# A hybrid decoder layer: order of the attention steps on four engines, and where the large buffers begin in on-chip memory

## The chip, the core and the metric

The kernel runs on one core of a Trainium2 chip. The metric is the device time of one execution in microseconds (us). Weights and activations come from HBM by DMA, work happens in SBUF (128 partitions, each with its own byte addresses), and TensorE writes its results to PSUM, which has eight banks of 2 KB in each partition.

## The reference, cut to what matters

One layer over 512 tokens of width 1024, all float32:

```
h    = RMSNorm(x)
proj = h @ w_in          # RWKV part | q | k | v | gate_A | gate_B
y_a  = rwkv7(...) @ w_up_a            # chunked recurrence, 8 heads of 64
y_b  = causal attention with ALiBi(q, k, v) @ w_up_b   # 8 heads of 64
x    = x + (sigmoid(gate_A) * y_a + sigmoid(gate_B) * y_b) @ w_o
h    = RMSNorm(x)
x    = x + (silu(h @ w_g) * (h @ w_u)) @ w_ffn_out     # hidden width 2816
out  = RMSNorm(x)
```

With 512 tokens and blocks of 256, at most one block is fully past, so the block-sparse attention is plain causal attention.

## The kernel before, in words

**Products in three parts.** Every large product is kept near float32 accuracy by splitting both operands into a rounded part (`_hi`) and a rest (`_lo`), both of type float32r. `three` (L1481) issues hi*hi (L1483), hi*lo (L1484) and lo*hi (L1485) into the same PSUM bank, each a matmul of 128 rows by 512 moving columns. The first operand of `pe.matmul(out, a, b)` is the stationary one (a weight load, LDWEIGHTS in the trace, goes ahead of each matmul), the second is the moving one. The names in a row of the trace are not in that order. One matmul loads 512 bytes of each partition as its stationary operand and streams 2,048 bytes of each partition as its moving one.

**Weight units.** The weights come in 147 units of 128x1024, numbered by stage: 3 LoRA units (the second and third with 80 columns a tile instead of 128), 12 for r, k, v, 4 for the attention's values (VB), 8 for its q and k (QK), 16 gate units (`U_GATE`), 8 up units, 8 for w_o, 44 for the FFN's first product, 22 for its second. SyncE (SP) loads a unit into `wraw` (2 slots, L454), ScalarE (ACT) rounds it into `w_hi` (`split_hi`, L755), VectorE (DVE) makes `w_lo` (`split_lo`, L1096; both with 4 slots), and TensorE takes it (`take`, L1498). A unit of the gates, LoRA, RKV, QK and the FFN's first product is 24 matmuls with `w` stationary and `hT` (the transposed h) moving. The VB units have `hT` stationary and `w` moving. The up stage (L1899) has `w` stationary and `yaT` or `obT` moving. w_o (`by_rows`, L1909) has `mixT` stationary and `w` moving; the FFN's second product (`down`, L1944) has `act` stationary and `w` moving.

**The attention stage** has 16 steps n, for four pairs of heads times four query tiles t = n mod 4 of 128 tokens. One gate unit goes with each step. In a step:
- `attn_scores` (L1820): two matmuls (four records in the trace) with 128(t+1) moving columns;
- DVE `score_bias` (L1348) adds the ALiBi row and keeps the maximum, ACT `probs` (L998) does the exponential and the sum, DVE `weights` (L1360) takes the reciprocal and scales;
- `probs_T` (L1838): 2(t+1) transposes, read out of PSUM by ACT's `probs_T` (L1008) into `PT`;
- `values` (L1849): the product with V, 4(t+1) records;
- `gate` (L1863): a half of the unit (12 matmuls) into PSUM bank 0, from which DVE `gate_copy` (L1374) copies the result. The first half of the next unit waits for that copy (L1870).
- at the end of four steps ACT's `ob_hi` (L1017) and DVE's `ob_lo` (L1369) take the pair's result out of bank 1.

The order is written out by hand for each engine. TensorE (L1880 to L1894) issues, in step m: first gate half, scores of m+1, transposes of m, second gate half, values of m. ACT (L1023) and DVE (L1386) follow loops of their own over the same m, and each of them also splits unit m+3.

**Addresses.** `sb` (L109) puts tensors one after the other, each at a multiple of 32 bytes, and `at[0]` is set back by hand where buffers share room. The first free byte of the program is 16,481, rounded to 16,512. `ident`, `blk1`, `par`, `omka` and `omu` take 512+512+256+32+64 bytes, so `hT_hi` begins at 17,888 = 8 x 2,048 + 1,504. `hT_lo`, `wraw`, `w_hi` and `w_lo` follow, each a multiple of 4,096 long. Then come `ss`, `rstd` and `warm` (160 bytes) and then `base` = 91,776 = 44 x 2,048 + 1,664, at which `yaT`, `act`, `obT`, `mixT` and nearly everything else begins, or a multiple of 2,048 later.

| group | tensors | start, modulo 2,048 | modulo 512 | modulo 64 |
|---|---|---|---|---|
| H | hT_hi, hT_lo, wraw, w_hi, w_lo | 1,504 | 480 | 32 |
| B | yaT, obT, mixT, act and the scratch from `base` on | 1,664 | 128 | 0 |

Of the kernel before, what the change touches and what calls it, by code (L numbers as in the profile page):

```python
# [39 lines left out]
P = 128  # L40
D = 1024
T = 512
KD = D // P
TT = T // P
HD = 64
AW = 512
NP_ = AW // P
# [25 lines left out]
U_GATE = 27  # L73
# [8 lines left out]
RKV_TILE = [4, 5, 6, 7, 0, 1, 2, 3, 8, 9, 10, 11]  # L82
VB_BANK = [7, 0, 5, 6]
FILL_BANK = [7, 3]
NRAW = 2
NSPL = 4
LEAD = 3
# [11 lines left out]
def build(nc, x, norm_mix_g, w_in, mu_shift, w0, w_decay_up, a0, w_iclr_up, w_gate_up, k_k, k_a, r_k,  # L99
# [6 lines left out]
    with ExitStack() as ctx:  # L106
        at = [(nc.sbuf_base + 31) // 32 * 32]

        def sb(name, shape, dt=F32):  # L109

            t = nc.alloc_sbuf_tensor_at(name, shape, dt, offset=at[0])
            n = 4
            for s in shape[1:]:
                n *= s
            at[0] += (n + 31) // 32 * 32
            assert at[0] <= nc.sbuf_usable_end, (name, at[0])
            return t
# [12 lines left out]
        t_dram = nc.dram_tensor("t_scratch", (NQ, NP_ * 2 * TT, QB, QB), F32).ap()  # L130
        omka = sb("omka", [P, 4])
        omu = sb("omu", [P, 16])
        hT_hi = sb("hT_hi", [P, KD, T], F32R)
        hT_lo = sb("hT_lo", [P, KD, T], F32R)
        wraw = sb("wraw", [P, NRAW, 1024])
        w_hi = sb("w_hi", [P, NSPL, 1024], F32R)
        w_lo = sb("w_lo", [P, NSPL, 1024], F32R)
        ss = sb("ss", [P, 3, TT])
        rstd = sb("rstd", [P, 3, TT])
        warm = sb("warm", [P, 4])  # L140
        base = at[0]


        yaT_hi = sb("yaT_hi", [P, NP_, T], F32R)
# [609 lines left out]
        def _(act):  # L754
            def split_hi(u, fourth):  # L755

                s = fourth % NRAW
                act.wait_ge(w_loaded[s], (u - fourth % NRAW) // NRAW * 32 + 32 if isinstance(u, int)
                            else (u - s) * (32 // NRAW) + 32)
                if not isinstance(u, int) or u >= NSPL:  # L760
                    act.wait_ge(w_used, u - NSPL + 1)
                n = unit_width(u)
                act.activation(w_hi[:, fourth % NSPL, 0:n], wraw[:, s, 0:n], ACT.Copy).then_inc(w_hi_ready, 1)  # L763
# [234 lines left out]
            def probs(m):  # L998
                n = P * (m % TT + 1)
                for e in range(2):  # L1000
                    act.wait_ge(sc_ready, 2 * m + e + 1)
                    if m >= 2:
                        act.wait_ge(pT_mm, 2 * (m - 2) + e + 1)
                        act.wait_ge(rrec_ready, m - 1)
                    act.activation(Pr[:, m % 2, e, 0:n], sc[:, m % 2, e, 0:n], ACT.Exp, bias=nmax[:, m % 2, e:e + 1],  # L1005
                                   scale=-1.0, accum_out=rsum[:, m % 2, e:e + 1]).then_inc(exp_ready, 1)

            def probs_T(m):  # L1008
                n = P * (m % TT + 1)
                for e in range(2):  # L1010
                    act.wait_ge(pT_mm, 2 * m + e + 1)
                    if m and e == 0:
                        act.wait_ge(pv_mm, m)
                    act.activation(PT[:, e].rearrange("p a b -> p (a b)")[:, 0:n], PS[:, 6 + e, 0:n], ACT.Copy)\
                       .then_inc(PT_ready, 1)

            def ob_hi(p):  # L1017
                act.wait_ge(pv_mm, TT * (p + 1))
                act.activation(obT_hi[:, p, :], PS[:, 1, :], ACT.Copy).then_inc(obhi_ready, 1)

            probs(0)
            ystd(TT - 1)
            for m in range(TT * NP_):  # L1023
                if m + 1 < TT * NP_:
                    probs(m + 1)
                probs_T(m)
                if m == 0:
                    y_affine(TT - 1)
                split_hi(U_GATE + m + LEAD, U_GATE + m + LEAD)
                if m == 1:  # L1030
                    ya_hi(TT - 1)
                if m % TT == TT - 1:
                    ob_hi(m // TT)


            act.wait_ge(gates_stored, 2 * KD)
# [50 lines left out]
        def _(dve):  # L1087
            n = [0]
# [7 lines left out]
            def split_lo(u, fourth):  # L1096

                s, q = fourth % NRAW, fourth % NSPL
                dve.wait_ge(w_hi_ready, u + 1)
                n = unit_width(u)  # L1100
                dve.tensor_tensor(w_lo[:, q, 0:n], wraw[:, s, 0:n], w_hi[:, q, 0:n].bitcast(F32), ALU.subtract)\  # L1101
                   .then_inc(w_lo_ready, 1)
# [245 lines left out]
            def score_bias(m):  # L1348

                w = P * (m % TT + 1)  # L1350
                for e in range(2):
                    dve.wait_ge(s_done, 2 * m + e + 1)
                    dve.wait_ge(alibi_ready, 2 * (m // TT) + e + 1)
                    if m >= 2:
                        dve.wait_ge(exp_ready, 2 * (m - 2) + e + 1)
                    dve.tensor_tensor_reduce(sc[:, m % 2, e, 0:w], PS[:, 2 + 2 * (m % 2) + e, 0:w],  # L1356
                                             alibi[:, e, T - w:T], 1.0, 3e38, ALU.add, ALU.min,
                                             nmax[:, m % 2, e:e + 1]).then_inc(sc_ready, 1)

            def weights(m):  # L1360
                n = P * (m % TT + 1)
                dve.wait_ge(exp_ready, 2 * m + 2)
                dve.reciprocal(rrec[:, m % 2, :], rsum[:, m % 2, :]).then_inc(rrec_ready, 1)
                dve.wait_ge(rrec_ready, m + 1)
                for e in range(2):
                    dve.tensor_scalar(Pr[:, m % 2, e, 0:n], Pr[:, m % 2, e, 0:n], rrec[:, m % 2, e:e + 1], None, ALU.mult)\
                       .then_inc(Pr_ready, 1)

            def ob_lo(p):  # L1369
                dve.wait_ge(obhi_ready, p + 1)  # L1370
                dve.tensor_tensor(obT_lo[:, p, :], PS[:, 1, :], obT_hi[:, p, :].bitcast(F32), ALU.subtract)\
                   .then_inc(oblo_ready, 1)

            def gate_copy(m):  # L1374
                dve.wait_ge(w_used, U_GATE + m + 1)
                dve.tensor_copy(gates[:, KD - 1 - m // 2, m % 2, :], PS[:, 0, :]).then_inc(gates_stored, 1)  # L1376
# [1 line left out]
            score_bias(0)  # L1378
            y_var(TT - 1)
            weights(0)  # L1380
            score_bias(1)
            y_rstd(TT - 1)
            gate_copy(0)
            weights(1)
            split_lo(U_GATE + LEAD, U_GATE + LEAD)
            for m in range(1, TT * NP_):  # L1386
                if m + 1 < TT * NP_:
                    score_bias(m + 1)
                    weights(m + 1)
                gate_copy(m)  # L1390
                split_lo(U_GATE + m + LEAD, U_GATE + m + LEAD)
                if m == 1:
                    ya_lo(TT - 1)
                if m % TT == TT - 1:
                    ob_lo(m // TT)


            def mix_lo(k):
# [81 lines left out]
        def _(pe):  # L1480
# [339 lines left out]
            def attn_scores(m):  # L1820
                p, t = m // TT, m % TT
                a = 2 * ((p + 1) % NP_)
                if t == 0:
                    pe.wait_ge(qk_loaded[p], 16)
                if m >= 2:
                    pe.wait_ge(sc_ready, 2 * (m - 2) + 2)
                elif m == 0:
                    pe.wait_ge(tok_ready, 3 * TT - 2)
                    pe.wait_ge(fill_ready, 2 * TT)
                else:  # L1830
                    pe.wait_ge(yc_ready, TT)
                    pe.wait_ge(G_ready, 2 * TT)
                for e in range(2):
                    r = slice(HD * e, HD * e + HD)
                    pe.matmul(PS[:, 2 + 2 * (m % 2) + e, 0:P * (t + 1)], qkT[r, a, t * P:(t + 1) * P],  # L1835
                              qkT[r, a + 1, 0:P * (t + 1)], start=True, stop=True).then_inc(s_done, 1)

            def probs_T(m):  # L1838
                for e in range(2):
                    pe.wait_ge(Pr_ready, 2 * m + e + 1)  # L1840
                    if m:
                        pe.wait_ge(PT_ready, 2 * (m - 1) + e + 1)
                    else:
                        pe.wait_ge(U_ready, 2 * TT)
                    for j in range(m % TT + 1):
                        ins = pe.transpose(PS[:, 6 + e, j * P:(j + 1) * P], Pr[:, m % 2, e, j * P:(j + 1) * P], ident[:])  # L1846
                    ins.then_inc(pT_mm, 1)
# [15 lines left out]
            def gate(n, half):  # L1863
# [13 lines left out]
                if half:  # L1877
                    ins.then_inc(w_used, 1)

            attn_scores(0)  # L1880
            for m in range(TT * NP_):
                gate(m, 0)
                if m + 1 < TT * NP_:
                    attn_scores(m + 1)
                if m == 0:
                    gate(0, 1)
                    probs_T(0)
                    y_T(TT - 1)
                else:
                    if m == 1:  # L1890
                        values(0)
                    probs_T(m)
                    gate(m, 1)
                    values(m)  # L1894


            pe.wait_ge(yalo_ready, TT)
# [90 lines left out]
```

## Time and profile before

| what | value |
|---|---|
| median of 3 runs | 885.13 us (884.59 to 888.14) |
| the profiled execution: its own time | 885.59 us |
| its span, first to last instruction | 883.9 us |
| granted TensorE clock, mean over the span | 0.995 |
| attention stage, first gate matmul to first matmul of the up stage | 284.20 to 414.03: 129.8 us |
| TensorE busy | 850.9 us (96% of the span) |
| VectorE, ScalarE, GpSimd busy | 411.5, 334.4, 118.6 us |
| HBM traffic over the span | 79 MB, 89 GB/s |

The execution's own time is 1.7 us longer than its span and 0.46 us over the median of the runs. TensorE's busy time is the union of matmul records whose ends are modelled and which overlap each other, so "96% busy" does not say how densely matmuls are issued: for that, starts are compared with starts. Two records of one stage with the number of matmuls between them give the mean distance from start to start, which is called the *gap* below.

### The profile page before, as it was taken

How to read it: one execution, taken by the hardware profiler on the slowest of the kernel's cores; microseconds unless marked ns; L12 is line 12 of the kernel's file. 1: busy time of each engine (PE TensorE's matmuls, PEld its weight loads, DVE VectorE, ACT ScalarE, POOL GpSimd, SP SyncE). 2: the span in 40 equal slices, each digit the busy share in tenths (PEclk: the TensorE clock that was granted, in tenths of full speed). 3: DMA queues.
4: the chain of work that ended last, by engine and by line, in shares of the span. 5: the costliest groups of instructions: out<-in, count | busy, mean ns of one | idle time of the engine just before them, and what ended most of it. 6: DMA issues, size and time to landing. Idle time of an engine off the chain costs nothing.

```text
span 883.9 us, 12041 instructions
## 1 busy us (share of the span) xinstructions
PE 850.9 (96%) x4561; PEld 670.5 (76%) x4561; DVE 411.5 (47%) x600; ACT 334.4 (38%) x512; POOL 118.6 (13%) x124
## 2 busy tenths in 40 slices
PE   5999999999999999999999899999999999999995
PEld 4677767778778677667888688888888888888884
DVE  5379677443452544544662464444444444222214
ACT  6568241322323533334431364444444444211122
POOL 3054850220222301100330000000000000000000
PEclk9999999999999999999999999999999999999998
DMA  6421441320115222122334233333333332222222
GB/s 199 121 72 49 108 130 45 88 72 14 37 37 166 73 73 70 50 72 72 95 133 158 67 95 95 95 95 95 95 95 95 96 104 95 102 90 90 92 70 95
DMA packets 122298, 79.45 MB, mean 90 GB/s; under 512 B 15033, under 2 KB 110322, under 8 KB 122258
## 3 DMA queue, kind: packets, MB, share of 16 engines
q1 hardware_dynamic: 122066, 78.87, 30.1%
q8 instruction: 28, 0.46, 0.2%
q14 instruction: 12, 0.10, 0.0%
q0 software_dynamic: 192, 0.02, 0.0%
HBM read 73.63 MB, written 5.24 MB: 89 GB/s over the span
## 4 chain that ended last, share of the span: by engine, by line
PE 87%; DVE 8%; ACT 3%; issue 1%; DMA 0%; POOL 0%; SPq 0%; ACTq 0%; DVEq 0%
PE PS L1483 25%; PE PS L1484 24%; PE PS L1485 24%; PE PS L1835 1%; PE PS L1579 1%; DVE sq L1175 1%; DVE w_lo L1101 1%; PE PS L1846 1%; PE PS L1684 1%; DVE gates L1376 1%; PE PS L1724 1%; PE PS L1723 1%; PE PS L1702 1%; PE PS L1762 1%; PE PS L1594 1%
## 5 line engine op out<-in xcount | busy, mean ns | idle before, releaser
L1483 PE MATMUL PS<-hT_hi,w_hi 128*128 128x512 f32 (+1 forms) x664 | 269.5, 406 | 8.7 <-DVE gates L1376 3.9
L1485 PE MATMUL PS<-hT_hi,w_lo 128*128 128x512 f32 (+1 forms) x664 | 259.9, 391 | 0.0
L1484 PE MATMUL PS<-hT_lo,w_hi 128*128 128x512 f32 (+1 forms) x664 | 259.6, 391 | 0.0
L1101 DVE TENSOR_TENSOR w_lo<-wraw,w_hi 128x1024 fp32r<-128x1024 f32 (+1 forms) x125 | 164.9, 1320 | 161.1 <-ACT w_hi L763 159.4
L763 ACT ACTIVATE w_hi<-wraw 128x1024 fp32r<-128x1024 f32 (+1 forms) x125 | 131.3, 1050 | 139.1 <-PE PS L1485 113.9
L1483 PEld LDWEIGHTS PS<-hT_hi,w_hi 128*128 128x128 f32 (+1 forms) x664 | 124.4, 187 | 44.8 <-issue 17.4
L1485 PEld LDWEIGHTS PS<-hT_hi,w_lo 128*128 128x128 f32 (+1 forms) x664 | 124.4, 187 | 27.4
L1484 PEld LDWEIGHTS PS<-hT_lo,w_hi 128*128 128x128 f32 (+1 forms) x664 | 124.7, 188 | 24.6 <-issue 1.0
L1484 PE MATMUL PS<-w_lo,act_hi 128*128 128x512 f32 x176 | 70.3, 399 | 0.0
L1483 PE MATMUL PS<-w_hi,act_hi 128*128 128x512 f32 x176 | 69.4, 394 | 0.0
L1485 PE MATMUL PS<-w_hi,act_lo 128*128 128x512 f32 x176 | 69.0, 392 | 0.0
L1071 ACT ACTIVATE act_hi<-prod 128x512 f32 x22 | 13.9, 632 | 103.4 <-DVE prod L1447 103.4
L1005 ACT ACTIVATE Pr<-sc,nmax 128x128 f32<-128x128 f32 (+3 forms) x32 | 17.7, 555 | 68.1 <-DVE nmax L1356 68.1
L1447 DVE TENSOR_TENSOR prod<-gact,PS 128x512 f32<-128x512 f32 x22 | 15.1, 688 | 57.7 <-PE PS L1485 57.7
L1483 PEld LDWEIGHTS PS<-w_hi,act_hi 128*128 128x128 f32 x176 | 33.0, 188 | 8.6
L1485 PEld LDWEIGHTS PS<-w_hi,act_lo 128*128 128x128 f32 x176 | 33.0, 188 | 7.9
L1484 PEld LDWEIGHTS PS<-w_lo,act_hi 128*128 128x128 f32 x176 | 33.0, 188 | 7.5
L1443 DVE TENSOR_TENSOR gact<-sgf,PS 128x512 f32<-128x512 f32 x22 | 15.1, 688 | 36.4 <-ACT sgf L1068 36.4
L1356 DVE CUSTOM_DVE_ANT_0 sc<-PS,alibi 128x128 f32<-128x128 f32 (+3 forms) x32 | 14.4, 488 | 34.3 <-PE PS L1835 34.2
L1068 ACT ACTIVATE sgf<-PS 128x512 f32<-128x512 f32 x22 | 13.2, 598 | 35.9 <-PE PS L1485 35.9
L1485 PE MATMUL PS<-w_hi,mixT_lo 128*128 128x512 f32 x64 | 25.5, 399 | 0.0
L1484 PE MATMUL PS<-w_lo,mixT_hi 128*128 128x512 f32 x64 | 25.2, 394 | 0.0
(237 smaller groups left out, 1044.6 us busy)
## 6 DMA issues: line engine op xcount, KB each, us to landing
wraw<-in_w_ffn_in_dram SPq DMA_DIRECT2D x88, 256.0 KB, 3.1
wraw<-in_w_in_dram SPq DMA_DIRECT2D x82, 256.0 KB, 3.3
wraw<-in_w_ffn_out_dram SPq DMA_DIRECT2D x44, 256.0 KB, 2.9
wraw<-in_w_o_dram SPq DMA_DIRECT2D x16, 256.0 KB, 3.0
xt<-in_x_dram SPq DMA_DIRECT2D x4, 512.0 KB, 4.9
qk_scratch<-stage SPq DMA_DIRECT2D x8, 256.0 KB, 3.0
qkT<-qk_scratch SPq DMA_DIRECT2D x4, 512.0 KB, 4.8
wraw<-in_w_up_a_dram SPq DMA_DIRECT2D x8, 256.0 KB, 3.1
```

Of the source, the lines that this page charges most:

```text
L763: act.activation(w_hi[:, fourth % NSPL, 0:n], wraw[:, s, 0:n], ACT.Copy).then_inc(w_hi_ready, 1)
L1005: act.activation(Pr[:, m % 2, e, 0:n], sc[:, m % 2, e, 0:n], ACT.Exp, bias=nmax[:, m % 2, e:e + 1], scale=-1.0, accum_out=rsum[:, m % 2, e ...
L1068: act.activation(sgf[:, j, :], PS[:, 2 * j, :], ACT.Sigmoid).then_inc(sgf_ready, 1)
L1071: act.activation(act_hi[:, bass.ds(2 * i + j, 1), :], prod[:, j:j + 1, :], ACT.Copy)\
L1101: dve.tensor_tensor(w_lo[:, q, 0:n], wraw[:, s, 0:n], w_hi[:, q, 0:n].bitcast(F32), ALU.subtract)\
L1175: dve.reciprocal(sq[:, p, :], sq[:, p, :]).then_inc(rinv_ready, 1)
L1356: dve.tensor_tensor_reduce(sc[:, m % 2, e, 0:w], PS[:, 2 + 2 * (m % 2) + e, 0:w], alibi[:, e, T - w:T], 1.0, 3e38, ALU.add, ALU.min, nmax[ ...
L1443: dve.tensor_tensor(gact[:, j, :], sgf[:, j, :], PS[:, 2 * j, :], ALU.mult).then_inc(gact_ready, 1)
L1447: dve.tensor_tensor(prod[:, j, :], gact[:, j, :], PS[:, 2 * j + 1, :], ALU.mult)\
L1483: pe.matmul(out_, a_hi, b_hi, start=start, stop=False)
L1484: pe.matmul(out_, a_hi, b_lo, start=False, stop=False)
L1485: return pe.matmul(out_, a_lo, b_hi, start=False, stop=stop)
```

## The change

**Steps of the attention.** TensorE now issues a gate unit as a whole, then scores of n+1, transposes of n and values of n-1 in one group; the last step keeps the unit in two halves. The values of a step therefore come one step later. ACT's and DVE's loops are put in a matching order: ACT does the transposes' copies ahead of the exponentials, DVE the gate copy ahead of the score bias, and `ob_hi` and `ob_lo` come one step later. DVE gets one more wait, in step 10, for the scores of step 11.

**Addresses.** `ss`, `rstd` and `warm` move ahead of `hT_hi`, and the allocator is rounded up to a multiple of 2,048 bytes there. `hT_hi` then begins at 18,432 = 9 x 2,048 and `base` at 92,160 = 45 x 2,048. Both groups of the table above begin at 0 modulo 2,048. `ident` and `blk1` ahead of them and `V_b` at the top of the memory stay where they are.

```diff
+ROW = 4 * T
...
+        ss = sb("ss", [P, 3, TT])
+        rstd = sb("rstd", [P, 3, TT])
+        warm = sb("warm", [P, 4])
+        at[0] = (at[0] + ROW - 1) // ROW * ROW
         hT_hi = sb("hT_hi", [P, KD, T], F32R)
...
-        ss = sb("ss", [P, 3, TT])
-        rstd = sb("rstd", [P, 3, TT])
-        warm = sb("warm", [P, 4])
         base = at[0]
+        assert base % ROW == 0
...
             probs(0)
             ystd(TT - 1)
-            for m in range(TT * NP_):
-                if m + 1 < TT * NP_:
-                    probs(m + 1)
-                probs_T(m)
-                if m == 0:
+            for n in range(TT * NP_):
+                probs_T(n)
+                if n and n % TT == 0:
+                    ob_hi(n // TT - 1)
+                if n == 0:
                     y_affine(TT - 1)
-                split_hi(U_GATE + m + LEAD, U_GATE + m + LEAD)
-                if m == 1:
+                if n + 1 < TT * NP_:
+                    probs(n + 1)
+                split_hi(U_GATE + n + LEAD, U_GATE + n + LEAD)
+                if n == 1:
                     ya_hi(TT - 1)
-                if m % TT == TT - 1:
-                    ob_hi(m // TT)
+            ob_hi(NP_ - 1)
...
             weights(0)
-            score_bias(1)
             y_rstd(TT - 1)
-            gate_copy(0)
-            weights(1)
-            split_lo(U_GATE + LEAD, U_GATE + LEAD)
-            for m in range(1, TT * NP_):
-                if m + 1 < TT * NP_:
-                    score_bias(m + 1)
-                    weights(m + 1)
-                gate_copy(m)
-                split_lo(U_GATE + m + LEAD, U_GATE + m + LEAD)
-                if m == 1:
+            for n in range(TT * NP_):
+                if n == 10:
+                    dve.wait_ge(s_done, 2 * n + 4)
+                gate_copy(n)
+                if n + 1 < TT * NP_:
+                    score_bias(n + 1)
+                if n and n % TT == 0:
+                    ob_lo(n // TT - 1)
+                if n + 1 < TT * NP_:
+                    weights(n + 1)
+                split_lo(U_GATE + n + LEAD, U_GATE + n + LEAD)
+                if n == 1:
                     ya_lo(TT - 1)
-                if m % TT == TT - 1:
-                    ob_lo(m // TT)
+            ob_lo(NP_ - 1)
...
+            N_STEP = TT * NP_
             attn_scores(0)
-            for m in range(TT * NP_):
-                gate(m, 0)
-                if m + 1 < TT * NP_:
-                    attn_scores(m + 1)
-                if m == 0:
-                    gate(0, 1)
-                    probs_T(0)
+            for n in range(N_STEP - 1):
+                gate(n, 0)
+                gate(n, 1)
+                attn_scores(n + 1)
+                probs_T(n)
+                if n:
+                    values(n - 1)
+                else:
                     y_T(TT - 1)
-                else:
-                    if m == 1:
-                        values(0)
-                    probs_T(m)
-                    gate(m, 1)
-                    values(m)
+            gate(N_STEP - 1, 0)
+            probs_T(N_STEP - 1)
+            values(N_STEP - 2)
+            gate(N_STEP - 1, 1)
+            values(N_STEP - 1)
```

## Rows read from the trace of the kernel before

**Rows 1.** The page: the chain of work that ended last, by engine.

```profile
PE 87%; DVE 8%; ACT 3%; issue 1%; DMA 0%; POOL 0%; SPq 0%; ACTq 0%; DVEq 0%
```

**Rows 2.** TensorE's timeline, matmuls at ends of stages: start us, us, engine, line, what.

```profile
414.03 0.49 PE L1483 MATMUL PS<-yaT_hi,w_hi 128*128 128x512 f32 x1 [0.19 <-issue]
...
459.10 0.40 PE L1483 MATMUL PS<-w_hi,mixT_hi 128*128 128x512 f32 x1
...
503.68 0.40 PE L1485 MATMUL PS<-w_hi,mixT_lo 128*128 128x512 f32 x1
...
517.69 0.39 PE L1483 MATMUL PS<-hT_hi,w_hi 128*128 128x512 f32 x1
...
751.62 0.39 PE L1483 MATMUL PS<-w_hi,act_hi 128*128 128x512 f32 x1
...
874.59 0.39 PE L1485 MATMUL PS<-w_hi,act_lo 128*128 128x512 f32 x1
```

**Rows 3.** The chain of waits, float32 products of the RWKV gate: start us, us.

```profile
121.86 6.87 PE PS L1762 x16
```

**Rows 4.** TensorE's timeline, steps 9 to 12 of the attention stage.

```profile
327.23 0.39 PE L1485 MATMUL PS<-hT_hi,w_lo 128*128 128x512 f32 x1
327.54 0.92 PE L1835 MATMUL PS<-qkT 64*128 64x384 f32 x4
328.39 0.66 PE L1846 MATMUL PS<-ident,Pr 128*128 128x128 f32 x4
328.80 0.48 PE L1483 MATMUL PS<-hT_hi,w_hi 128*128 128x512 f32 x1
329.12 0.39 PE L1484 MATMUL PS<-hT_lo,w_hi 128*128 128x512 f32 x1
...
331.75 0.66 PE L1858 MATMUL PS<-PT,V_b 128*64 128x128 f32 x8
332.69 0.47 PE L1483 MATMUL PS<-hT_hi,w_hi 128*128 128x512 f32 x1 [0.29 <-DVE gates L1376]
...
340.19 0.88 PE L1858 MATMUL PS<-PT,V_b 128*64 128x128 f32 x12
341.40 0.47 PE L1483 MATMUL PS<-hT_hi,w_hi 128*128 128x512 f32 x1 [0.34 <-DVE gates L1376]
...
348.50 1.09 PE L1858 MATMUL PS<-PT,V_b 128*64 128x128 f32 x16
349.52 0.50 PE L1483 MATMUL PS<-hT_hi,w_hi 128*128 128x512 f32 x1
...
356.23 0.44 PE L1858 MATMUL PS<-PT,V_b 128*64 128x128 f32 x4
357.18 0.47 PE L1483 MATMUL PS<-hT_hi,w_hi 128*128 128x512 f32 x1 [0.51 <-DVE gates L1376]
```

**Rows 5.** DVE's timeline, the step with 512 columns of scores.

```profile
336.75 0.69 DVE L1356 CUSTOM_DVE_ANT_0 sc<-PS,alibi 128x512 f32<-128x512 f32 x1 [3.08 <-PE PS L1835]
...
339.24 1.42 DVE L1366 TENSOR_SCALAR Pr<-Pr,rrec 128x512 f32<-128x512 f32 x2
340.58 0.68 DVE L1376 COPY gates<-PS 128x512 f32<-128x512 f32 x1
341.18 1.21 DVE L1101 TENSOR_TENSOR w_lo<-wraw,w_hi 128x1024 fp32r<-128x1024 f32 x1
```

**Rows 6.** ACT's timeline, the same step.

```profile
338.21 0.71 ACT L1005 ACTIVATE Pr<-sc,nmax 128x512 f32<-128x512 f32 x1
...
338.91 0.85 ACT L1014 ACTIVATE PT<-PS 128x384 f32<-128x384 f32 x2
339.65 1.06 ACT L763 ACTIVATE w_hi<-wraw 128x1024 fp32r<-128x1024 f32 x1
```

**Rows 7.** GpSimd's timeline, and the waits of the attention stage.

```profile
338.15 3.11 POOL L742 TENSOR_SCALAR alibi<-alibi 128x512 f32<-128x512 f32 x2 [29.42 <-DVE nmax L1356]
...
PE PS L1483 <- DVE gates L1376: 3.9, 11, 0.5
```

## The prediction, on record before the changed kernel ran

> **What bounds the kernel now.** I read the page's chain of work first: TensorE holds 87% of the chain that ended last [rows 1]. So what counts is how densely TensorE issues. A busy share can't say that, because records overlap, so I took starts against starts in its timeline [rows 2]. The FFN's first product without its first unit: 43 units x 24 = 1,032 matmuls from 517.69 to 751.62 us, 233.93/1,032 = 0.2267 us from start to start. The FFN's second product: 528 matmuls, so 527 gaps from 751.62 to 874.59, 122.97/527 = 0.2333. w_o: 192 matmuls, 191 gaps from 459.10 to 503.68, 0.2334. The up stage: 192 gaps from 414.03 to 459.10, 0.2347. All four stages issue the same matmul (512 moving columns, 128x128 stationary, float32r), and nothing waits inside them, yet three are 3% slower. What differs is where the operands begin: in the fast stage both are of group H (480 modulo 512), in the slow ones one is of H and the other of B (128 modulo 512).
>
> Then the attention stage, also start against start [rows 4]. A gate half meets a seam on both sides: the first gap after other work is 329.12 - 328.80 = 0.32, the last before other work 327.54 - 327.23 = 0.31, each 0.08 to 0.09 over 0.227. And after `values` TensorE waits for DVE's copy of bank 0: the waits table puts 3.9 us of it in 11 waits on that copy [rows 7].
>
> **The order of the attention, by parts of the sum.** Per step t, from `values` to the next gate: 0.95 for 4 records (356.23 to 357.18), 0.94 for 8, 1.21 for 12, 1.02 for 16 [rows 4]. Only the 16 run without a wait, at 0.055 a record and 0.14 for the seams; the others would then take 0.36, 0.58 and 0.80. So the wait costs 0.59 + 0.36 + 0.41 + 0 = 1.36 in four steps, more than the table's idle time, which counts from modelled ends. In the new order scores, transposes and the last step's values stand between the end of a unit and the next unit. For t = 1 that is 0.85 + 0.41 + 0.36 = 1.6 us [rows 4], the least of the four. The copy takes 0.68 [rows 5] and can start when the last gate matmul's record of 0.39 has ended [rows 4], so bank 0 is free 1.1 us after that matmul's start. It is hidden in every step: remove 1.36. One half fewer: remove both its seams, 0.17 x 4 = 0.68. Added: transposes are followed by values instead of a gate matmul. That seam isn't in this trace; the two ends are a transposes' own spacing (about 0.11) and the wait-bound seam from values to gate (about 0.20), against 0.03 which transposes to gate takes. So 0.08 to 0.17 x 4 = 0.3 to 0.7 added. Net 1.3 to 1.7 in four steps. 15 of 16 steps are fused: x 3.75 = 5.0 to 6.5. I take 5.6.
>
> What is moved past what: DVE's step of 512 columns is copy 0.68, score bias 2 x 0.69, weights 1.42, `split_lo` 1.21 [rows 5], with reciprocal and reads some 5 of the 8 us of a step. After the start of the scores, the chain to the next transposes is now longer: scores, transposes and values about 1.1 + 0.7 + 0.6 by the rows of t = 1 and their sizes, ACT's copies 0.85, two exponentials at 0.70 from start to start (338.21 to 338.91) plus a tail, 1.8 in all [rows 6], then 0.2 + 1.42, about 6.7 us. The next transposes come at 8.5 (a unit of 24 x 0.227 + 0.17, the 2.4, and the next scores): slack 1.8. `split_lo` then ends at about 8, when the next copy becomes ready; if it is 0.3 late, the 2.4 us ahead of the next unit take it. `split_hi` and the splits are for unit n+3, three steps ahead, so SP's loads (released by `split_lo`) keep over a step of slack. GpSimd's two ALiBi rows, 3.1 us [rows 7], start after the score bias of t = 3, now computed at the end of the previous step, and are wanted a step later. `ob_hi` and `ob_lo` fall in steps with few columns. The wait of step 10 holds the copy until the scores of step 11 are done, about 1.1 us after they start by the 0.85 of 384 columns [rows 4]; the copy then ends at 1.9, and the unit comes at 2.4: nothing. All these at 0; if the cover of the copy went, 1.36 per four steps would come back.
>
> **The addresses.** Both groups move to residue 0. Then H against B has the relation that H against H has today. If the relation is what costs, the slow stages come down to 0.2267: up 192 x 0.0080 = 1.5, w_o 192 x 0.0067 = 1.3, second product 528 x 0.0067 = 3.5, together 6.3 us. The unknown is the absolute residue. H is at 32 modulo 64, so today no float32r matmul has both operands at a multiple of 64. For: TensorE's float32 products of the RWKV gate have both operands in B, and their records of 512 columns are 6.87/16 = 0.429 apart [rows 3]; if a record is two passes, that is 0.2147 a pass, with next to nothing for the change of weights. Against: in the up stage the moving operand alone is at a multiple of 64, in the second product the stationary one alone, and both are slower, not faster, than with neither. The row nearest is the FFN's first product, same type and same relation, so I take 0.2267 unchanged for the other 2,088 matmuls; the bounds are 0.2147 (36 us less over 3,000) and 0.2333 (14 us more).
>
> Sum, against the profiled execution (885.59, its span of 883.9 and 1.7 around it): 885.59 - 5.6 - 6.3 = 873.7. The median of the runs is 0.46 lower: **873.2 us**.
>
> The row shows one gap of 0.2267 and one of 0.2333 for equal matmuls. The Trainium skill, "SBUF — State Buffer", section "Who interferes with whom", says that TensorE has two independent read ports, one for the moving operand and one for the weight load, and that it never waits on anyone. By that rule the addresses would change nothing: it is the second rival below. The 3% between stages speak against it.
>
> **The rivals.**
> - *The absolute residue costs too* (0.24). For: the float32 row. Against: one-sided alignment gains nothing today. If each gap falls to 0.220 (half way to that row), 3,000 x 0.0067 = 20 us more go: 853. At 0.2147 it is 837. On the Trainium skill's page "TensorE: Matmul & The Clock Gate", section "Wait — 56ns, not 53.3ns?", 512 columns are 215.7 ns apart; by that the estimate is 840.
> - *Addresses change nothing* (0.13): the 3% come from which buffer streams, not from where it begins. Then only the order counts: 885.13 - 5.6 = 879.5.
> - *The order gains nothing* (0.08). Weights of DVE come after ACT's longer queue, and the transposes wait for them: the slack of 1.8 turns into a wait of 0.4 a step. Then 885.13 - 6.3 = 878.8.
> - *Slower: equal starts collide* (0.09). Stationary and moving operand both begin at 0 modulo 2,048 and meet in the same place of the memory in every matmul. The first product's gap then goes to the second's, 2,088 x 0.0066 = +13.8, and nothing is won in the others: 885.1 - 5.6 + 13.8 = 893.3. Against: in H both share a residue already. It decides from a mean gap of (2,088 x 0.2267 + 912 x 0.2336 + 5.6)/3,000 = 0.2307 on.
>
> **How the numbers follow.** Forecast 0.46, rivals 0.24, 0.13, 0.08, 0.09. The range 850 to 882 holds the forecast with its bounds, both rivals at 879, and the nearer half of the first: 0.46 + 0.13 + 0.08 + 0.12 = 0.79. It leaves out gaps under 0.219 and the collision. A measurement can tell about 0.5% (4.4 us) from no change. Faster by more than that: forecast and first rival whole, most of the two at 879 (0.6 to 0.7% faster): 0.82. Same: the rest of these, 0.10. Slower: 0.08.
>
> **What would show it.** Right: first and second product of the FFN, w_o and up all at 0.226 to 0.228 from start to start; the attention stage at 124 us (129.8 in the table of the times); no wait of L1483 for the gate copy; transposes to values 0.11 to 0.20. Wrong: a gap of 0.216 to 0.222 in all stages (first rival), 0.2333 left in the second product (second rival), idle time of the transposes with DVE's L1366 as releaser (third), 0.233 in the first product (the last).

## The result and the profile after

The changed kernel takes 874.28 us (median of 4 runs, 871.28 to 876.62) beside 886.60 for the kernel before (4 runs, 884.59 to 888.14). The ratio is 0.986, 95% interval 0.983 to 0.990. Forecast was 873.2, within 850 to 882. The profiled execution of after took 876.54 us, span 874.8, so it is 2.3 us above its median, and 2.8 above the 873.7 that the sum gave for a profiled execution. Most of that is accounted for below.

The profile's page of the changed kernel: its span, and the shares of the chain.

```profile
span 874.8 us, 12042 instructions
...
PE 89%; DVE 6%; ACT 3%; DMA 1%; issue 1%; POOL 0%; SPq 0%; ACTq 0%; DVEq 0%
```

TensorE held 87% of the chain before [rows 1] and holds 89% now: the same bound, with less around it. The timeline of TensorE after, at the ends of the stages (first gate matmul, first of up, of w_o, its last, first of the FFN's second product, the last of all), against [rows 2]:

```profile
285.14 0.50 PE L1487 MATMUL PS<-hT_hi,w_hi 128*128 128x512 f32 x1
...
410.60 0.49 PE L1487 MATMUL PS<-yaT_hi,w_hi 128*128 128x512 f32 x1 [0.15 <-issue]
...
454.24 0.39 PE L1487 MATMUL PS<-w_hi,mixT_hi 128*128 128x512 f32 x1
...
497.53 0.39 PE L1489 MATMUL PS<-w_hi,mixT_lo 128*128 128x512 f32 x1
...
747.08 0.39 PE L1487 MATMUL PS<-w_hi,act_hi 128*128 128x512 f32 x1
...
866.53 0.39 PE L1489 MATMUL PS<-w_hi,act_lo 128*128 128x512 f32 x1
```

Start against start, as the prediction did it: up 43.64/192 = 0.2273, w_o 43.29/191 = 0.2267, second product 119.45/527 = 0.2267. The first product keeps its 0.2267 (233.92 us for its 1,032). Four stages now have one gap. The up stage's 0.2273 holds one first gap of 0.33; inside, it is 0.2267.

The span by stages, from a first matmul to the next first matmul:

| stretch | before | after | difference |
|---|---|---|---|
| start to first gate matmul | 284.20 | 285.14 | +0.94 |
| attention | 129.83 | 125.46 | -4.37 |
| up | 45.07 | 43.64 | -1.43 |
| w_o, to the first transpose of the norm | 48.33 | 47.12 | -1.21 |
| norm, first transpose to first FFN matmul | 4.73 | 6.27 | +1.54 |
| FFN, first product | 239.46 | 239.45 | 0 |
| FFN, second product | 122.97 | 119.45 | -3.52 |
| behind the last matmul's start | 9.27 | 8.28 | -0.99 |

The sum is -9.0, the difference of the two spans 9.1. Of the +0.94, 0.95 had been lost by the first product of all (its first matmul starts at 17.86 instead of 16.91); it has to do with neither part of the change that I can name.

Step 5 of the attention (steps count from 0) in the timeline after, from the last matmul of the gate unit to the second of the next; and behind it the first gate matmul four steps on from that of step 5, which starts at 323.26. By this count the rows from before [rows 4] are of steps 5 to 8, and not 9 to 12 as their heading has it:

```profile
328.62 0.39 PE L1489 MATMUL PS<-hT_hi,w_lo 128*128 128x512 f32 x1
328.94 0.92 PE L1839 MATMUL PS<-qkT 64*128 64x384 f32 x4
...
330.38 0.44 PE L1862 MATMUL PS<-PT,V_b 128*64 128x128 f32 x4
330.75 0.50 PE L1487 MATMUL PS<-hT_hi,w_hi 128*128 128x512 f32 x1
331.08 0.39 PE L1488 MATMUL PS<-hT_lo,w_hi 128*128 128x512 f32 x1
...
354.50 0.50 PE L1487 MATMUL PS<-hT_hi,w_hi 128*128 128x512 f32 x1
```

`values` with 4 records now lead to the gate in 0.37 us (330.38 to 330.75), where it took 0.95 [rows 4]. The group starts 0.32 behind the unit's last matmul; before it was 0.31. The last gap of the list is 331.08 - 330.75 = 0.33; before, behind the wait for the copy, it was 0.31 (332.69 to 333.00). Four steps take 354.50 - 323.26 = 31.24 us, against 349.52 - 317.00 = 32.52 before: 1.28 less.

The waits of the attention stage after (total us, times, longest):

```profile
ACT PT L1017 <- PE PS L1862: 67.8, 15, 5.3
...
DVE gates L1380 <- PE PS L1489: 20.7, 14, 3.4
```

The row `PE PS L1483 <- DVE gates L1376: 3.9, 11, 0.5` [rows 7] has no counterpart. What waits now is DVE's gate copy on TensorE and ACT's copy of the transposes. Both engines have time: these waits cost nothing. TensorE has one new wait, in step 15, where no scores and no values stand between the first gate half and the transposes:

```profile
404.58 1.09 PE L1850 MATMUL PS<-ident,Pr 128*128 128x128 f32 x8 [0.20 <-DVE Pr L1370]
```

The transposes start 0.59 us behind the last gate matmul (403.99) instead of 0.32, and what ended the wait is DVE's `weights` of that step.

Step 10, with the added wait of DVE:

```profile
369.52 0.66 PE L1862 MATMUL PS<-PT,V_b 128*64 128x128 f32 x8
370.11 0.50 PE L1487 MATMUL PS<-hT_hi,w_hi 128*128 128x512 f32 x1
```

0.59 us for 8 records, and 370.44 for the second gate matmul: no wait. The added wait keeps the gate copy off memory that the scores of step 11 still read, and delays nothing.

The norm between w_o and the FFN, in the timeline after and in the windows view (the stretch and its length, busy time and count of PE, PEld, DVE, ACT, POOL, then the granted clock, DMA share and GB/s):

```profile
501.36 5.38 PE L1517 MATMUL PS<-ident,xn 128*128 128x128 f32 x32 [3.44 <-DVE x L1428]
...
507.63 0.47 PE L1487 MATMUL PS<-hT_hi,w_hi 128*128 128x512 f32 x1 [0.89 <-DVE hT_lo L1129]
```

```profile
502.00:505.50 3.50, 3.50 (x20) 3.50 (x18) 2.88 (x5) 1.80 (x4) 0.00 (x0) 0.52 0.00 0
```

The same place before:

```profile
507.43 3.84 PE L1513 MATMUL PS<-ident,xn 128*128 128x128 f32 x32 [3.35 <-DVE x L1424]
...
512.16 0.47 PE L1483 MATMUL PS<-hT_hi,w_hi 128*128 128x512 f32 x1 [0.89 <-DVE hT_lo L1125]
```

After 3.44 us in which TensorE waited for DVE, the granted clock fell: it is 0.52 over this stretch, so the lower level (1.2 GHz) for nearly all of it, and the 32 transposes took 5.38 us instead of 3.84. Before, with a wait of 3.35 us, the clock stayed at the higher level.

### The profile page after: what moved, and what is told of

The parts are those of the page before. It is cut to its first block, busy times and chain, and to the rows that moved or that the text cites. A ratio compares the mean times of both kernels' runs of the same rounds, so it can differ in the third digit from the quotient of the medians.

```text
span 874.8 us, 12042 instructions
## 1 busy us (share of the span) xinstructions
PE 845.1 (97%) x4561; PEld 672.9 (77%) x4561; DVE 411.1 (47%) x600; ACT 334.1 (38%) x512; POOL 117.2 (13%) x124
## 4 chain that ended last, share of the span: by engine, by line
PE 89%; DVE 6%; ACT 3%; DMA 1%; issue 1%; POOL 0%; SPq 0%; ACTq 0%; DVEq 0%
PE PS L1487 25%; PE PS L1489 24%; PE PS L1488 24%; PE PS L1839 1%; PE PS L1850 1%; PE PS L1862 1%; PE PS L1583 1%; DVE sq L1179 1%; DVE w_lo L1105 1%; PE PS L1517 1%; PE PS L1688 1%; PE PS L1728 1%; PE PS L1706 1%; PE PS L1727 1%; DMA xt<-in_x_dram 1%; PE PS L1766 1%
## 5 line engine op out<-in xcount | busy, mean ns | idle before, releaser
L1488 PE MATMUL PS<-w_lo,act_hi 128*128 128x512 f32 x176 | 68.5, 389 | 0.0
L1017 ACT ACTIVATE PT<-PS 128x128 f32<-128x128 f32 (+3 forms) x32 | 12.3, 435 | 70.5 <-PE PS L1862 67.8
L1487 PE MATMUL PS<-w_hi,mixT_hi 128*128 128x512 f32 x64 | 24.9, 389 | 0.0
```

Source lines behind the costliest of these rows:

```text
L1487: pe.matmul(out_, a_hi, b_hi, start=start, stop=False)
L1488: pe.matmul(out_, a_hi, b_lo, start=False, stop=False)
```

## The experiments

Theory A: what costs 3% is the relation between the addresses of the two operands of a matmul. Rival B: it is where each begins, whatever the other does. Theory C: the order gains by the removed wait for the gate copy, and gives part back at the seams.

**Each part alone.** The first run is the kernel before with these lines alone (with `4 * T` written out for `ROW`), the second is the changed kernel with them undone.

```diff
+        ss = sb("ss", [P, 3, TT])
+        rstd = sb("rstd", [P, 3, TT])
+        warm = sb("warm", [P, 4])
+        at[0] = (at[0] + ROW - 1) // ROW * ROW
         hT_hi = sb("hT_hi", [P, KD, T], F32R)
...
-        ss = sb("ss", [P, 3, TT])
-        rstd = sb("rstd", [P, 3, TT])
-        warm = sb("warm", [P, 4])
```

> The order of before, both groups of buffers at 0 modulo 2,048. If the two parts add up: every float32r stage at a gap of 0.2267, up, w_o and second product together 6.3 us shorter, the attention stage unchanged at about 129.8 us; about 879 against 885.6. If the new order needs the addresses or the other way round, the up stage or the attention stage differs from this.

> The new order, the addresses of before. Expected: attention stage 125.5 us as in the changed kernel (it was 129.8), gaps of the up stage, w_o and the second product back at 0.2347, 0.2334 and 0.2333; about 881. If the gaps depend on which buffer streams and not on addresses they would be 0.2267 here too, and then the addresses were not the cause.

Addresses only: 881.13 us, ratio 0.994 (0.992 to 0.996). Order only: 881.01 us, 0.994 (0.992 to 0.996). By the medians 5.6 and 5.8 us under 886.8; the product of the two ratios, 0.988, lies inside the change's own interval. Addresses only, the timeline of TensorE from the first of up on:

```profile
414.89 0.49 PE L1484 MATMUL PS<-yaT_hi,w_hi 128*128 128x512 f32 x1 [0.18 <-issue]
...
751.24 0.39 PE L1484 MATMUL PS<-w_hi,act_hi 128*128 128x512 f32 x1
...
870.69 0.39 PE L1486 MATMUL PS<-w_hi,act_lo 128*128 128x512 f32 x1
```

Order only:

```profile
284.55 0.50 PE L1485 MATMUL PS<-hT_hi,w_hi 128*128 128x512 f32 x1
...
409.97 0.49 PE L1485 MATMUL PS<-yaT_hi,w_hi 128*128 128x512 f32 x1
...
747.56 0.39 PE L1485 MATMUL PS<-w_hi,act_hi 128*128 128x512 f32 x1
...
870.53 0.39 PE L1487 MATMUL PS<-w_hi,act_lo 128*128 128x512 f32 x1
```

The second product is 119.45 us with the new addresses and 122.97 with the old. The attention stage is 409.97 - 284.55 = 125.42 with the new order, and 129.93 with the old one at the new addresses. Each part does its work in its own stages, and neither touches the other's.

**Relation or place.** Both groups at 1,696 modulo 2,048, that is 32 modulo 64, which is where H lay modulo 64 before.

```diff
-        at[0] = (at[0] + ROW - 1) // ROW * ROW
+        at[0] += 32
```

> The changed kernel with its two groups both at 1,696 modulo 2,048 (32 modulo 64) and not at 0. If only the relation of the operands counts: 0.2267 in all four stages, the time of the changed kernel. If multiples of 64 or of 2 KB count: the up stage, w_o and second product back at 0.230 to 0.235, 3 to 6 us longer.

```profile
412.65 0.49 PE L1487 MATMUL PS<-yaT_hi,w_hi 128*128 128x512 f32 x1
...
456.31 0.39 PE L1487 MATMUL PS<-w_hi,mixT_hi 128*128 128x512 f32 x1
...
749.15 0.39 PE L1487 MATMUL PS<-w_hi,act_hi 128*128 128x512 f32 x1
...
868.60 0.39 PE L1489 MATMUL PS<-w_hi,act_lo 128*128 128x512 f32 x1
```

Up 43.66, second product 119.45: the same gaps as at 0 modulo 2,048. So A holds and B falls: for these matmuls the rounding to 2 KB matters only because it makes the two groups equal. Yet the time is 878.29 us, 0.991 (0.988 to 0.995), 4 us over the changed kernel. The attention stage (125.41) and all behind it are as fast as there; this execution begins the attention 2.1 us later. The loss lies around the product for the attention's V (the issues of DMA with KB each and median us from issue to landing, then the timelines of ACT and TensorE):

```profile
m_scratch<-Mfull SPq DMA_DIRECT2D x4, 128.0 KB, 3.2
...
113.79 1.06 ACT L766 ACTIVATE w_hi<-wraw 128x1024 fp32r<-128x1024 f32 x1 [8.77 <-DMA wraw<-in_w_in_dram]
...
117.64 0.47 PE L1487 MATMUL PS<-w_hi,hT_hi 128*128 128x512 f32 x1 [2.47 <-issue]
```

SyncE issues four stores of `Mfull`, a tensor of group B, waits for them, issues a load back into group B (`Mb`), and only then the next weights. The stores take 3.2 us from issue to landing, where the changed kernel has 2.6. ACT waits 8.77 us for the weights (6.71 there), TensorE stands still for 2.47 us ahead of the product (0.42 there), and at 118.6 us the granted clock falls to the lower level (0.70 in the mean of 117 to 121 us), so that it takes 44.9 us from this matmul to the first transposes of `rkvT` instead of 43.3. Two later runs, which shift the operands of B, bear this out. The stores take 3.2 us in the three runs whose group B begins at no multiple of 128 bytes (here, and 64 and 32 bytes past one), and 2.6 to 2.7 in the ten others; with the shift of 32 TensorE's wait is 2.44 us and the clock falls at the same place, with the shift of 64 it is 1.54 us and the clock stays up. So the addresses of B have a part in the 4 us, by way of the DMA and not of the matmuls. How much of the 4 us in the medians this is isn't shown, since this kernel has one trace; nor is it shown why such stores take longer.

**The seam behind the transposes.** The values of n-1 are issued ahead of the transposes of n, so that transposes and not values stand before the gate.

```diff
                 attn_scores(n + 1)
-                probs_T(n)
                 if n:
                     values(n - 1)
-                else:
+                probs_T(n)
+                if n == 0:
                     y_T(TT - 1)
             gate(N_STEP - 1, 0)
-            probs_T(N_STEP - 1)
             values(N_STEP - 2)
+            probs_T(N_STEP - 1)
             gate(N_STEP - 1, 1)
```

> The changed kernel with the values of n-1 issued ahead of the transposes of n. The seam from transposes to values (0.20) and the one from values to the gate unit (0.20, first gap 0.336) become one from values to transposes (0.20) and one from transposes to the gate unit (0.03, first gap 0.315). If seams belong to pairs of instructions: 0.19 less a step, 2.8 us less in 15 steps, attention stage 122.6. If the transposes' seams depend on what DVE and ACT have ready: no gain, or a wait for Pr. Rival: bank 0 is free later than the group ends; a wait for the gate copy would then show.

```profile
341.67 0.39 PE L1489 MATMUL PS<-hT_hi,w_lo 128*128 128x512 f32 x1
341.99 0.49 PE L1839 MATMUL PS<-qkT 64*128 64x128 f32 x4
342.41 0.88 PE L1862 MATMUL PS<-PT,V_b 128*64 128x128 f32 x12
343.22 1.09 PE L1850 MATMUL PS<-ident,Pr 128*128 128x128 f32 x8
344.06 0.48 PE L1487 MATMUL PS<-hT_hi,w_hi 128*128 128x512 f32 x1
344.38 0.39 PE L1488 MATMUL PS<-hT_lo,w_hi 128*128 128x512 f32 x1
```

871.24 us, ratio 0.982 (0.978 to 0.985); the stage takes 122.0 us, 3.46 less than in the changed kernel, where 2.8 were expected. From the last transpose to the gate it is 0.03, where the changed kernel has 0.20 from values to gate, and the gate's first gap is 0.32 (344.38 - 344.06) instead of 0.33. With the whole gate unit, which is 0.04 shorter in the mean of four steps, that is 0.21 a step, 3.2 in 15 steps. The rest is step 15: the values now stand ahead of its transposes, and the wait for DVE's `weights` is gone. Run again beside the changed kernel on one chip:

> The kernel of e4 once more beside e7 and the changed kernel on one chip: 871, and 0.983 of the kernel before.

> The changed kernel on the same chip: 874, 2.8 to 3 us over e9.

869.73 us (0.982, 0.980 to 0.985) beside 873.96 (0.986, 0.984 to 0.988): 4.2 us by the medians. The order with transposes last beats the kernel before clearly. Over the changed kernel the two intervals just overlap; what shows its gain is the stage itself, 3.5 us shorter in both pairs of traces.

**How equal must the starts be?** On the changed kernel, H stays at 0 and the four operands of group B are shifted, each by its own amount: first by 64 (yaT), 256 (obT), 384 (mixT) and 64 (act), then by 32, 128, 320 and 32. The diff is that of the first run; `mixers` and `mixed` lie 64 and 256 further already (`stage`, not shown, moves with yaT).

```diff
+        at[0] += 64
         yaT_hi = sb("yaT_hi", [P, NP_, T], F32R)
...
-        at[0] = mixers
+        at[0] = mixers + 192
         obT_hi = sb("obT_hi", [P, NP_, T], F32R)
...
-        at[0] = mixed
+        at[0] = mixed + 128
         mixT_hi = sb("mixT_hi", [P, KD, T], F32R)
...
-        at[0] = base
+        at[0] = base + 64
         act_hi = sb("act_hi", [P, FT, T], F32R)
```

> The changed kernel (H at 0) with yaT at 64, obT at 256, mixT at 384 and act at 64 bytes past a multiple of 2,048. If operands need an equal residue modulo 512: all of these stages at 0.229 to 0.235. If the relation counts modulo 64 alone: all at 0.2267. If modulo 256: obT at 0.2267, the others over it.

> The same with yaT at 32, obT at 128, mixT at 320 and act at 32. By a relation modulo 64: yaT and act slow (0.233 or more), obT and mixT at 0.2267. By a relation modulo 256 or 512: all of them over 0.2267.

The timeline with shifts of 64, 256, 384 and 64:

```profile
410.12 0.50 PE L1488 MATMUL PS<-yaT_hi,w_hi 128*128 128x512 f32 x1 [0.15 <-issue]
...
454.44 0.40 PE L1488 MATMUL PS<-w_hi,mixT_hi 128*128 128x512 f32 x1
...
748.30 0.40 PE L1488 MATMUL PS<-w_hi,act_hi 128*128 128x512 f32 x1
...
871.27 0.39 PE L1490 MATMUL PS<-w_hi,act_lo 128*128 128x512 f32 x1
```

The up stage takes 44.32 us, 0.2308 a matmul with its seams, and the second product 122.97/527 = 0.2333, which is what both kernels with the old addresses have. Each half of the up stage, yaT and obT, has its own gap, in both runs:

| operand of B | its part | shift, gap | shift, gap |
|---|---|---|---|
| yaT | moving | 64, 0.2302 | 32, 0.2332 |
| obT | moving | 256, 0.2308 | 128, 0.2330 |
| mixT | stationary | 384, 0.2324 | 320, 0.2333 |
| act | stationary | 64, 0.2333 | 32, 0.2333 |
| none (FFN, first product) | | 0, 0.2267 | 0, 0.2267 |

A single run each: 881.28 and 883.43 us, beside 886.43 before. No shift gives 0.2267, not even one of 256: for these matmuls equality is wanted modulo 512, and being equal modulo 64 isn't enough. In between there are steps (0.2302 for 64, 0.2308 for 256) for which these runs give no law.

**The tiles of 80 columns.** LoRA units 2 and 3 load 320 bytes for each matmul, 320 bytes apart. Their gap is 0.2300 in the kernel before. If equal starts are the rule, tiles 512 bytes apart should give 0.2267. This and the next two runs stand on the order with transposes last.

```diff
-                n = unit_width(u)
+                n = unit_width(u) // KD
+                def part(t):
+                    return t.rearrange("p (k c) -> p k c", k=KD)[:, :, 0:n]
...
-                    w = slice((k0 + k) * width, (k0 + k + 1) * width)
+                    w = slice((k0 + k) * P, (k0 + k) * P + width)
```

> The kernel of e4 with the 80-column tiles of the second and third LoRA unit laid 512 bytes apart and not 320. If an equal residue modulo 512 is what gives 0.2267: the gaps of these 48 matmuls fall from a mean of 0.2301 to 0.2267, 0.16 us less, not to be seen in the time of a run. If narrow tiles are slow in themselves: 0.2301 again.

```profile
23.32 0.40 PE L1493 MATMUL PS<-hT_hi,w_hi 128*80 128x512 f32 x1
...
34.52 0.39 PE L1493 MATMUL PS<-hT_hi,w_hi 128*128 128x512 f32 x1
```

A miss: 11.20/48 = 0.2333 (871.84 us, a single run). Equal starts are here, and the full 3% too. What differs from all the fast matmuls of 128 columns is where the load ends: 320 modulo 512 instead of 0. The last run shifts the tiles within their 512 bytes, by 192 bytes for unit 2 (so the load ends at 512) and by 96 for unit 3 (it ends at 416). `off(u)` is 48 elements for unit 2, 24 for unit 3 and 0 for all others, and stands in the load and in both splits too.

```diff
-                    w = slice((k0 + k) * P, (k0 + k) * P + width)
+                    w = slice((k0 + k) * P + off(u), (k0 + k) * P + off(u) + width)
```

> e8 again (80-column tiles 512 bytes apart), but a tile begins 192 bytes behind its multiple of 512 in the second LoRA unit, so that its 320 bytes end at the next multiple, and 96 bytes behind in the third. e8 gave 0.2334 with the start at 0. If what has to fit the moving operand's start is where the weight load ends: 0.2267 in the second unit, more in the third. If it is where the load starts: both over 0.2267. If narrow tiles are slow in themselves: both 0.233.

```profile
21.96 0.39 PE L1497 MATMUL PS<-hT_hi,w_hi 128*80 128x512 f32 x1
...
27.41 0.39 PE L1497 MATMUL PS<-hT_hi,w_hi 128*80 128x512 f32 x1
...
32.96 0.39 PE L1497 MATMUL PS<-hT_hi,w_hi 128*128 128x512 f32 x1
```

Unit 2: 5.45/24 = 0.2271, single gaps of 0.226 to 0.227. Unit 3: 5.55/24 = 0.2312. So equal starts are not the rule; where the weight load *ends* fits both widths. For a load of 512 bytes that is its start too, modulo 512, which is why the prediction's rule worked. But modulo 512 is not the whole of it. In the kernel before, the tiles of 320 bytes end 320, 128, 448, 256, 64, 384, 192 and 0 bytes past the moving operand's start, modulo 512. The fourth, which ends 256 past it, is as fast as the eighth:

```profile
26.15 0.39 PE L1483 MATMUL PS<-hT_hi,w_hi 128*80 128x512 f32 x1
...
26.83 0.40 PE L1483 MATMUL PS<-hT_hi,w_hi 128*80 128x512 f32 x1
```

0.68/3 = 0.227, where the first three tiles have 0.235, 0.230 and 0.229, and the second four tiles repeat the first. So for loads of 320 bytes an end that is equal modulo 256 is enough, while a load of 512 bytes was slow at 256 (obT, 0.2308). With one narrow width a rule of the end can't be told from one of the start (192 bytes past, modulo 256); that it is the end is argued from the 512-byte loads, not shown. 868.84 us in a single run is no verdict on the 0.3 us that unit 2 gains.

**The clock in the norm.** Ten more matmuls, into a bank that nobody reads, as the parts of x arrive.

```diff
+            for n in (1, 3):
+                pe.wait_ge(x2_ready, n)
+                for _ in range(5):
+                    pe.matmul(PS[:, 4, :], mixT_hi[:, 0, 0:P], mixT_hi[:, 0, :], start=True, stop=True)
             pe.wait_ge(x2_ready, TT)
```

> The kernel of e4 with ten matmuls more in TensorE's wait for the second norm, into a bank that DVE has read (their result is overwritten). If TensorE's 3.4 us without work ahead of the transposes are what lets its clock fall to 1.2 GHz there: no stretch at half clock, 4.7 us from the first transpose to the FFN's first matmul as in the kernel before and not 6.3, 1.6 us less in runs in which it fell. If the clock falls there whatever TensorE does: 6.3 us again, at the same place.

```profile
497.09 3.85 PE L1517 MATMUL PS<-ident,xn 128*128 128x128 f32 x32 [0.97 <-DVE x L1428]
...
501.83 0.47 PE L1487 MATMUL PS<-hT_hi,w_hi 128*128 128x512 f32 x1 [0.89 <-DVE hT_lo L1129]
```

```profile
496.50:502.00 5.50, 4.02 (x33) 3.66 (x34) 4.80 (x10) 4.18 (x9) 0.00 (x0) 1.00 0.00 0
```

Without the ten, in the repeated run of the same order:

```profile
496.95 5.38 PE L1517 MATMUL PS<-ident,xn 128*128 128x128 f32 x32 [3.44 <-DVE x L1428]
...
503.12 0.47 PE L1487 MATMUL PS<-hT_hi,w_hi 128*128 128x512 f32 x1 [0.79 <-DVE hT_lo L1129]
```

With them the granted clock is 1.00 throughout and the stretch takes 4.74 us instead of 6.17. The median is 868.87 (0.982, 0.979 to 0.984), 0.9 under the run without. The shorter stretch is measured; the gain in the total is not, since the intervals overlap. That the ten matmuls kept the clock up rests on one trace, and of the eight traces with a wait of 3.44 us and no extra matmuls one kept the higher clock too: it is likely, not shown.

## Why the prediction was right, and where its terms were off

**The addresses** were right in every stage. Forecast: up 1.5, w_o 1.3, second product 3.5. Measured in the table above: 1.43, 1.21, 3.52, together 6.2 against 6.3. The step "if the relation is what costs" was only a condition in the prediction. Both groups at 1,696 showed it: other residue, same 0.2267. What the prediction took for the relation, equal starts, is right for loads of 512 bytes alone. The choice to leave the other 2,088 matmuls at 0.2267 was right as well.

The Trainium skill, "SBUF — State Buffer", section "Who interferes with whom", has two independent read ports and a TensorE that never waits. Row and rule disagree here: 0.2267 and 0.2333 for equal matmuls of one kernel, and the shifts move a stage from one to the other. The measurement decides: 6.2 us of this kernel.

**Rival one, the absolute residue costs too,** had the chance 0.24 and fell. At 0 modulo 2,048 and at 32 modulo 64 the gap is the same. (The absolute address of group B does cost, but in DMA stores, which no rival had.) The float32 row [rows 3] that spoke for it, 0.2147 a pass, doesn't carry over to float32r. The Trainium skill, "TensorE: Matmul & The Clock Gate", section "Wait — 56ns, not 53.3ns?", gives 215.7 ns for 512 columns; no float32r stage of any run here came under 226.7.

**Rival two, addresses change nothing,** falls by the run with the addresses alone: 0.994 (0.992 to 0.996). **The rival that ends slower**, equal starts that collide, falls by the first product: 0.2267 stayed.

**The order:** forecast 5.6, measured 4.4 in the changed kernel and 129.83 - 125.42 = 4.4 in the run with the order alone. The mechanism was right: the 1.36 of wait per four steps went, and the cover that hides the copy held in all 16 steps. The third rival, with its 0.4 us a step of waiting for the weights, came in step 15 alone, where the cover of the transposes is one gate half. The size of two terms was off. The step "0.08 to 0.17 x 4 = 0.3 to 0.7 added" took the seam transposes to values between two ends; it is 0.20, the upper end, so 0.7 was added and the net is 1.34. The rows show 1.28; the other 0.06 lies in the gate's first gap, 0.31 behind a wait for the copy before and 0.33 to 0.34 behind values now, which the prediction didn't cost. Then "x 3.75" gives 1.28 x 3.75 = 4.8. The last 0.4 lies in the last four steps. The wait in step 15 costs 0.27 (0.59 instead of 0.32). And the wait for the copy behind the values of step 14 had been smaller from the start, 0.94 from values to gate instead of the 1.21 of the other steps with 12 records, so that 0.27 less could be won. The prediction had both ends of this seam from rows and took the middle; and it didn't ask what the other order would give, in which transposes stand before the gate: another 3.5 us.

**Not in the forecast:** the profiled execution of after lost 1.54 us in the norm to the lower clock, and 0.94 ahead of the attention, and won 0.99 behind the last matmul. With 1.2 of the order and 0.1 of the addresses this is 2.8, the distance between 873.7 and 876.54. The medians (873.2 forecast, 874.28 measured) lie closer, since the other runs include executions with a higher mean clock: the two near 871.7 us have 0.997, the two near 876.6 have 0.994. A miss of only 1.1 us is thus in part luck: the order was 1.2 too high, and which way the clock went was not in the sum.

**Costed at nothing, and at nothing in the attention stage:** the wait of step 10, GpSimd's ALiBi rows, the splits and SP's loads. None shows there as a wait of TensorE.

## What to carry to other kernels

When equal matmuls run at different distances from start to start, compare where the moving operand begins with where the weight load ends, modulo 512 bytes; make them equal, by one rounding in the allocator, and round to a multiple of 128 at least, since small DMA stores out of the same buffers were slower (3.2 us for 2.6) from other addresses. When small matmuls are grouped to hide a copy, count every seam between kinds, put the kind whose seam is cheapest next to the big product, and measure both orders. And read the granted clock of the stretch behind each wait of TensorE, since a kernel that gets faster elsewhere can lose it there.

## What the hardware showed that I had not expected

- The gap doesn't go by equal starts: tiles of 320 bytes that start with the moving operand have 0.2333, those that end with it, modulo 512, have 0.2271, and those that end 256 past it 0.227 too. For unequal addresses it takes values between (0.2302, 0.2308, 0.2312, 0.2324), which these runs don't explain. Nor do they say why 0.2267 and not less is the floor.
- At the lower clock, in the start of the kernel, gaps of 512 columns are 0.427; at the higher one 0.2267 is the best, more than half of that.
- The fall of the clock in the norm hangs on little. With a wait of 3.44 us it fell in seven of eight profiled executions (once with the old order); with 3.34 to 3.35 us it fell in one of four. The two with the old addresses are among those without a fall. Whether the addresses have a part in it, by the 0.1 us of the wait, stays open. The length of one wait alone doesn't decide it either: at 118.6 us the clock fell behind waits of 2.44 and 2.47.
- Seams between kinds of matmul differ by a factor: 0.03 from transposes to a gate matmul, 0.20 from transposes to values, from values to transposes and from values to gate.
